# Hybrid and forget-gate attention: the first filling piece runs ahead of the first scores, one later step goes without a piece

## The reference

```python
def hybrid_conv_mla(h, ...):                       # 8 heads, 64 + 32 features, causal
    z = h @ w_in                                   # u, gate_c, gate_b, cq, ckv, kr
    y_conv = gate_b * short_conv(gate_c * u, conv_w)
    q = rms_norm(cq, q_norm) @ w_uq                # nope part, rope part
    kv = rms_norm(ckv, kv_norm) @ w_ukv            # k_nope, v
    y_att = mla_attention(q_nope, rope(q_rope), k_nope, rope(kr), v)
    return concatenate([y_conv, y_att]) @ w_out

def forget_attention(q, k, v, log_f):              # 12 heads of 64, causal, q and k rms-normed
    c = cumsum(log_f)
    s = q @ k.T * scale + (c[t] - c[s])
    return softmax(s) @ v
# beside it 4 heads of attention into 256 memory tokens: memory_attention(mq, mk, mv)
# h = h + concatenate([forget, memory]) @ fox_w_out
```

## Time and profile before

| | before |
|---|---|
| median of three runs | 3099.71 us (3097.51 to 3101.0) |
| the profiled execution | 3098.23 us, its span 3096.4 us |
| TensorE busy (matmuls) | 3009.0 us, 97% |
| VectorE busy | 2331.3 us, 75% |
| ScalarE busy | 1719.8 us, 56% |
| hybrid attention | about 302 to 364 us of the span |
| forget-gate attention | about 1190 to 1296 us of the span |

### The profile page before, as it was taken

One profiled execution on the slowest core, in us unless ns is written; L12 is line 12 of the kernel. 1 busy time (PEld: TensorE's weight loads), 2 busy tenths in 40 slices (PEclk: granted clock), 3 DMA queues, 4 the chain that ended last, 5 costly groups with the idle time before them and its releaser, 6 DMA issues.

```text
span 3096.4 us, 48541 instructions
## 1 busy us (share of the span) xinstructions
PE 3009.0 (97%) x20737; PEld 2758.7 (89%) x20737; DVE 2331.3 (75%) x2678; ACT 1719.8 (56%) x1967; POOL 74.0 (2%) x143
## 2 busy tenths in 40 slices
PE   9999999999989999899989999999999999999999
PEld 8999899999879998899988888888888888899999
DVE  6887778788657567654677888888898888766675
ACT  5435443544435445444646777777777777555453
POOL 0110001010000000000000000000000000000000
PEclk9999999999999999999999999999999999999999
DMA  8885468686613543255315999999999899533353
GB/s 335 291 310 199 157 255 301 221 300 239 211 55 143 215 167 136 76 197 191 137 62 213 364 348 343 366 347 336 367 350 360 339 355 366 213 123 123 123 199 115
DMA packets 112381, 739.27 MB, mean 239 GB/s; under 512 B 12480, under 2 KB 12480, under 8 KB 32160
## 3 DMA queue, kind: packets, MB, share of 16 engines
q1 hardware_dynamic: 92304, 662.77, 57.3%
q0 software_dynamic: 19856, 73.34, 6.7%
HBM read 735.01 MB, written 1.05 MB: 238 GB/s over the span
## 4 chain that ended last, share of the span: by engine, by line
PE 81%; DVE 9%; DMA 4%; ACT 4%; issue 2%; SPq 0%; DVEq 0%; ACTq 0%
PE ps L559 60%; PE ps L558 19%; DMA ring<-in_w 3%; DVE wlo L2977 3%; ACT whi L1984 2%; PE ps L568 2%; DVE AF L2956 1%; DVE att L2965 1%; DVE T L2947 0%; DVE gf L2959 0%; DVE hl L2947 0%; DVE AF L2947 0%; ACT cv L1969 0%; DMA ring<-in_r 0%; DVE cv L2956 0%
## 5 line engine op out<-in xcount | busy, mean ns | idle before, releaser
L2977 DVE TENSOR_TENSOR wlo<-ring,whi 128x2048 fp32r<-128x2048 f32 x620 | 1416.3, 2290 | 404.0 <-ACT whi L1984 403.3
L1984 ACT ACTIVATE whi<-ring 128x2048 fp32r<-128x2048 f32 x620 | 1184.5, 1914 | 330.5 <-issue 168.6
L559 PE MATMUL ps<-whi,AR 128*128 128x512 f32 (+1 forms) x2884 | 911.3, 392 | 0.3 <-DVE AF L2947 0.3
L559 PE MATMUL ps<-hh,whi 128*128 128x256 f32 x2336 | 660.8, 283 | 0.0
L559 PE MATMUL ps<-hl,whi 128*128 128x256 f32 x2336 | 653.3, 280 | 0.0
L559 PE MATMUL ps<-hh,wlo 128*128 128x256 f32 x2336 | 653.1, 280 | 0.0
L559 PEld LDWEIGHTS ps<-whi,AR 128*128 128x128 f32 x2884 | 535.5, 188 | 115.5 <-issue 0.8
L559 PE MATMUL ps<-wlo,AR 128*128 128x512 f32 (+1 forms) x1442 | 556.9, 386 | 0.0
L559 PEld LDWEIGHTS ps<-hh,whi 128*128 128x128 f32 x2336 | 439.0, 188 | 5.1 <-issue 1.8
L559 PEld LDWEIGHTS ps<-hl,whi 128*128 128x128 f32 x2336 | 439.0, 188 | 1.5 <-issue 1.0
L559 PEld LDWEIGHTS ps<-hh,wlo 128*128 128x128 f32 x2336 | 438.5, 188 | 0.5
(11 more groups left out here) (268 smaller groups left out, 3392.6 us busy)
## 6 DMA issues: line engine op xcount, KB each, us to landing
ring<-in_w SPq DMA_DIRECT2D x620, 1024.0 KB, 5.0
rring<-in_r POOLq DMA_DIRECT2D x135, 512.0 KB, 4.8
first<-in_r SPq DMA_DIRECT2D x8, 512.0 KB, 18.4
ring<-in_r SPq DMA_DIRECT2D x4, 512.0 KB, 8.0
rring<-in_r SPq DMA_DIRECT2D x3, 512.0 KB, 17.4
AF<-in_mem SPq DMA_DIRECT2D x1, 1024.0 KB, 7.6
X<-in_x SPq DMA_DIRECT2D x1, 1024.0 KB, 16.3
AF<-in_cst POOLq DMA_DIRECT2D x1, 1024.0 KB, 5.3
```

The source lines that it names most:

```text
L559: return self.e.matmul(out, l, r, start=start, stop=stop)
L1984: self.e.activation(N.whi[:, c % HB, :], N.ring[:, c % RING, :], ACT.Copy).then_inc(N.sem["hi"], 1)
L2977: self.e.tensor_tensor(N.wlo[:, c % HB, :], N.ring[:, c % RING, :], N.whi[:, c % HB, :].bitcast(F32), ALU.subtract).then_inc(N.sem["lo"], 1)
```

## The change

attend on TensorE gets a switch `lead`, which issues one step of the filling generator ahead of scores(0). Both stages set it. All later pieces thereby stand one step earlier. In hybrid a bare yield behind the last input projection puts ada_sums and all that follows back into its old step, so that step 5 has ada_sums and no piece. In fox the bare yield stands behind the mark ("fox", "in"), so that step 9 has no piece and step 10 is as before. In fox the two sums of squares move as well: fk2 was ahead of queries 2's first piece and is now behind it; fq2 was ahead of values 2's first piece and is now behind it. The lists of the other four engines are the same.

```diff
--- before.py
+++ after.py
@@ -950,7 +950,7 @@
             self.need_mod(*coef)
         self.new_x()
 
-    def attend(self, parts, fill=None, late={}, order=None):
+    def attend(self, parts, fill=None, late={}, order=None, lead=False):
 
 
 
@@ -1010,6 +1010,8 @@
                     t = self.mm(b[:, o:o + sh.dv], PT[0:sz, n % 2, c:c + P], p.fns["v"](i, kb), x == 0, x == len(mine) - 1)
             t.then_inc(*self.up((p.key, "o", i), ("att", "o", self.heads + n)))
 
+        if lead:
+            next(fill)
         for n in range(len(seq) + 2):
             if n < len(seq):
                 scores(n)
@@ -1091,6 +1093,7 @@
             yield
             yield_all(gb2)
             self.mark("hy_in")
+            yield
             self.ada_sums(groups[0])
             yield
             for i in range(2):
@@ -1107,7 +1110,7 @@
         self.base, self.acc = 0, N.gs
         self.attend([Heads("hyat", HYBRID, q=lambda h: [N.h_qn[:, h // 2, :], N.h_qr[:, h // 4, :]], k=keys,
                            v=lambda h, kb: N.h_vn[:, kb, h * 64:h * 64 + 64], ready=ready,
-                           vready=lambda h: self.wait_ge("act", ("hy", "v", 1)))], conv_side())
+                           vready=lambda h: self.wait_ge("act", ("hy", "v", 1)))], conv_side(), lead=True)
         self.base = 4
         self.to_T("hyT", N.T2, 0, 4, "hyo", 4, [("hyat", "nat", 0), ("hyat", "nat", 1)])
         self.out_proj("hyout", "hy_w_out", "hyo", coef=(0, 5), parts=(2,))
@@ -1458,21 +1461,22 @@
             yield from val(1)
             yield from lin("k", 2)
             q2 = lin("q", 2)
+            next(q2)
             self.wide_sum("fk2", N.C("pairs"), [N.x_sq["fk2"]])
-            next(q2)
             yield
             next(q2)
             next(q2, None)
             yield
-            self.wide_sum("fq2", N.C("pairs"), [N.x_sq["fq2"]])
             v2 = val(2)
             next(v2)
+            self.wide_sum("fq2", N.C("pairs"), [N.x_sq["fq2"]])
             yield
             next(v2)
             next(v2, None)
             yield
             yield from lin("mq", 0)
             self.mark(("fox", "in"))
+            yield
             self.base, self.span = 5, 1
             self.wide_sum("fm", N.C("pairs"), [N.x_sq["fm"]])
             out0 = self.out_steps("foxout", "fox_w_out_2", "foxo", 0)
@@ -1501,7 +1505,7 @@
                            vready=lambda h: self.wait_ge("act", ("fox", "v", h // 4, 1)),
                            extra=lambda h: (N.ident[:, h:h + 1].to_broadcast([P, P]), N.x_ncT)),
                      self.mem_heads(0, N.x_mq, [N.x_mq2[:, j, :] for j in range(2)], "fm")], rest(),
-                    {9: lambda: turned(0, 5), 11: lambda: turned(1, 5), 14: lambda: turned(2, 5)})
+                    {9: lambda: turned(0, 5), 11: lambda: turned(1, 5), 14: lambda: turned(2, 5)}, lead=True)
         self.base, self.span = 4, 4
         turned(3)
         yield_all(self.out_steps("foxout", "fox_w_out_2", "foxo", 3))
```

## The result

| | before | changed |
|---|---|---|
| median of 20 runs each | 3100.45 us | 3106.32 us |
| lowest and highest | 3094.93 to 3107.12 us | 3101.59 to 3113.65 us |
| ratio of the times | | 1.0018, 95% interval 1.001 to 1.0025 |
| span of the profiled execution | 3096.4 us | 3104.7 us |

A forecast was written before the change was run, and what follows sets the result against it. TensorE, busy 3009.0 of 3096.4 us, was taken as the bound. Hybrid 0, forget gate +5.0 and clock falls 3.4 + 0.7 made +9.1 us on the 3099.71 us median: 3108.8 us, range 3102.3 to 3112.0.

The forecast's parts named there:

- rival A: Both stages: same waits, fewer clock falls, +5.0 or +6.7 us, or +3.3; 3103.0 to 3106.4 us, chance 0.31.
- the 6.2: Whole kernel: slower by over 6.2 us, about 0.2%, the least a measurement can tell; chance 0.69.
- The sum of 9.1 us: Whole kernel: hybrid 0, forget gate +5.0, clock falls 3.4 and 0.7 us, added to the median for 3108.8 us.
- The two led pieces: First scores of both stages: 2.9 us pieces in gaps of 2.73 and 2.56 us give no time by themselves.
- Hybrid 0: Hybrid step 5 without a piece: VectorE's chain sets the first output piece; worth 0, from -0.6 to +0.2 us.
- First sum: Forget gate, keys 2 sum of squares: TensorE waits 2.5 us for ScalarE's square, making flip(2) 3.5 us late.
- second: Forget gate, queries 2 sum of squares: TensorE waits 4.2 us for ScalarE's square, making flip(4) 7.0 us late.
- What comes back: Forget gate from step 9: the missing piece and earlier mark cut the 7.0 us delay to 5.0 us.
- The clock: Clock falls behind new waits: 3.4 us in the forget gate, 0.7 in hybrid; none regained from filled gaps.
- the forecast with both falls: Main case, clock falling behind both new forget-gate waits: 3107 to 3111 us, chance 0.57.
- B: Both empty steps: TensorE is the late engine and each gives its piece; -5.4 us, 3094.3 us, chance 0.05.
- C: Forget gate: sums wait but existing TensorE waits swallow the delay; 3099.7 us, between -1 and +2, chance 0.07.

The follow-up runs named there:

- E1: Changed kernel with the forget-gate part taken out, hybrid part alone: 3098.26 us against 3098.39 before, ratio 0.9996.
- E8: Changed kernel plus unread constant-data matmuls in TensorE's three long forget-gate waits: 3102.41 us against 3100.91 for the kernel before, ratio 1.0003.
- E3: Changed kernel with both sums of squares back in their old steps: 3095.47 us against 3098.39 for the kernel before, ratio 0.9983.
- E4: Changed kernel with ScalarE squaring keys 2 and queries 2 one step earlier: 3096.32 us against 3098.39 for the kernel before, ratio 0.9986.
- E6: Changed kernel with only the keys 2 sum of squares back in its old place: 3100.70 us against 3100.91 before, ratio 1.0003.
- E7: Changed kernel with only the queries 2 sum of squares back in its old place: 3103.24 us against 3100.91 before, ratio 1.0002.
- E10: Kernel before with both sums of squares one step earlier, no led piece or empty step: 3109.69 us against 3100.14 before, ratio 1.0026.
- E5: Kernel before with only the "fox in" mark counted earlier, behind the last projection piece: 3099.71 us against 3100.91, ratio 0.9994.
- E11: Kernel before plus changed hybrid part; forget gate with led piece, earlier mark, step 3 without a piece, sums unmoved: 3099.92 us against 3100.14, ratio 1.0000.
- E2: Changed kernel with the hybrid part taken out, forget-gate part alone: 3108.33 us against 3098.39 before, ratio 1.0028.
- E9: Changed kernel, both sums of squares in old steps, unread matmuls in one hybrid and one forget-gate wait: 3096.61 us against 3100.14 before, ratio 0.9985.

## Why the prediction was right

- **The time.** 3106.32 us lies in the range of 3102.3 to 3112.0, and the way that it came is the one foreseen. It lies just below the forecast's own band (3107 to 3111, chance 0.57) and in that of rival A (3103.0 to 3106.4, chance 0.31), and the 5.9 us stay under the 6.2 for which I gave 0.69. The sum of 9.1 us was 3.2 too high; the terms below say where.
- **The two led pieces give nothing by themselves.** Held: scores(0) of the forget gate start 6.6 us into the stage in the changed kernel, 6.5 before.
- **Hybrid 0.** Held for the mechanism: flip(4) is set by VectorE's copy, the output piece by its chain. The clock term of 0.7 us was right in kind: 0 where the wait was 2.0 us, and 0.5 to 1.3 us, 1.0 in the mean, in the six traces where it was 2.57 us or more. E1's median can't tell it from nothing.
- **First sum, 3.5 us; second, 7.0 us.** Held: waits of 2.50 and 4.22 us against 2.5 and 4.2, flip(6) 7.05 us late without falls (E8), and E3, E4, E6, E7 and E10 leave no other cause than ScalarE's order against TensorE's.
- **What comes back.** I had 7.0 less 5.0, so 2.0 us. It is 2.7: the stretch from flip(6) on is 55.5 us against 58.2. E5 gives 1.3 to 1.6 of it to the mark alone. The rest goes to the empty step: without it that stretch is 56.6 us (E5, E11), with it 55.5 to 55.6 (the changed kernel, E3). So the forget gate costs 4.4 us with the clock as before (116.4 less 110.4 less the fall of 1.6), not 5.0.
- **The clock, 3.4 + 0.7 us.** The price of a fall was right (1.6 to 1.7 us, by E2 and E8), the count was the mis-sized term: I reckoned with a fall behind each of the three new waits and with none removed. Behind the keys' sum the clock fell in three of four traces and not in that of the changed kernel, whose +6.0 us stretch has one fall more than before. How many come in one execution is chance, and so is how near the sum comes to it. And I took the two filled gaps to cost no clock, since they did not in one execution of before. E5 and E10 show that they sometimes do, at 1.6 us in the forget gate and 2.4 to 2.5 in hybrid; filling them gives that back. Worked out from these counts the sum is about 4.4 + 1.6 + 0.75 x 1.7 + 0.75 x 1.0 = 8.0 us with the new falls (queries' sum, keys' sum, hybrid), less 0.5 x 2.4 + 0.25 x 1.6 = 1.6 for those removed: 6.4 us, against 5.9 measured. That last step is argued from counts in few traces, not shown; counted in the same way E2 comes to 6.9 us, against 9.9 measured.

Of the rivals, A (the same waits, fewer falls) is nearest to what the changed kernel's own trace shows, at +6.7; the forecast with both falls is E2's trace. B and C are out: no empty step gave its piece, and the waits were not swallowed.

The Trainium skill's page "TensorE: Matmul & The Clock Gate", section "HAM oscillation — how this bites in real kernels", lets only long gaps bring the clock down. The changed kernel's two attention stages would nearly fit it: falls behind 4.22 and 3.43 us, none behind 2.50 and 1.99. The rest disagrees, for gaps of 1.9 to 2.6 us, behind which the clock fell in some executions and not in others of the same code: behind the hybrid stage's wait for flip(2), 1.9 to 2.05 us long, in 7 of 13 traces, the changed kernel's among them. Its section "What's actually happening" says that the same kernel differs from run to run in how many matmuls run at the low clock at its start; these traces show such differences behind waits in mid-kernel.

## What to carry to other kernels

A step moved in one engine's list must be held against the lists of the others: ask when its input is written there, and what stands in front of that. What a wait then costs is set by what is queued behind the waiting instruction, here flip, values and scores, for which VectorE waits. Work that fills a gap gives time only if the place it leaves is one where its engine is late, and an engine without idle ahead of an instruction may be there at the same moment as the one it would otherwise wait for (E11). A wait that can't be removed is a place for matmuls that hold the clock: 1.6 to 1.7 us for each fall avoided here (E8, E9).

## What the runs showed of the hardware

- The clock's fall behind a wait is not decided by the code alone. In four kernels whose instructions are the same up to there (before, E2, E5, E10), waits of 2.73 to 2.78 us at the same instruction were followed by a fall in two of four traces (mean granted clock 0.57 and 0.54 around the restart, against 1.00). Of all 13 traces, waits of about 2.0 us ahead of hybrid's flip(2) were followed by a fall in 7 traces, those of 2.4 to 3.4 us ahead of flip(6) in all 11 that had one.
- A fall cost 1.6 to 1.7 us where flip, values and scores behind it are on the chain, nearly the same after a wait of 2.4 as after one of 4.2 us (E2, E7, E8, E9). Once, behind E2's second sum, the clock stayed low longer (0.50 from 1227.92 to 1234.20), and the fall cost 3.0 us.
- Behind all five waits that were filled with unread matmuls (E8, E9) the granted clock was 1.00, and the next work started within 0.1 us of where it was. This is clear at flip(6), 2 of 2 filled against 0 of 11 unfilled, and weaker at the two sums, where 1 of 4 (keys 2) and 1 of 4 (queries 2) kept it without filling. At hybrid's flip(4) waits of 2.0 us kept it unfilled too.
